# Regrouping side products, a fifth weight bank and remainders on GpSimd in a 1010-unit weight-streaming kernel

## The reference

```python
def first_block(x, ...):
    x = x + lru_mlstm_layer(rmsnorm(x, e_norm[j]), ...)   # gated linear recurrence + 4-head matrix LSTM
    x = x + ssd_layer(rmsnorm(x, o_norm[j]), ...)         # state-space layer, 8 groups of 8 heads
    return rmsnorm(x, final_norm)

def second_block(x, ...):
    proj = rmsnorm_2(x, norm_mix_w) @ w_in
    # s5_branch, gla_branch (linear attention), diff_attn_branch, mixed by sigmoid gates
    h = x + merged @ w_out
    h = h + conv_gated_mlp(rmsnorm_2(h, norm_ffn_w), ffn_w_up, ..., ffn_w_down)
    return rmsnorm_2(h, norm_final_w)
```

## Time and profile before

| | |
|---|---|
| median of 3 runs | 3103.22 us (3101.56 to 3103.56) |
| profiled execution | 3104.65 us, span 3102.9 us |
| PE busy | 3037.9 us, 98% |
| DVE busy | 2312.4 us, 75% |
| ACT busy | 1763.4 us, 57% |
| POOL busy | 540.0 us, 17% |
| DMA, mean | 181 GB/s |
| chain that ended last | PE 85%, DVE 9%, ACT 3% |

### The profile page before, as it was taken

One profiled execution on the slowest core, in us unless ns is written; L12 is line 12 of the kernel. 1 busy time (PEld: TensorE's weight loads), 2 busy tenths in 40 slices (PEclk: granted clock), 3 DMA queues, 4 the chain that ended last, 5 costly groups with the idle time before them and its releaser, 6 DMA issues.

```text
span 3102.9 us, 53505 instructions
## 1 busy us (share of the span) xinstructions
PE 3037.9 (98%) x21726; PEld 2817.8 (91%) x21726; DVE 2312.4 (75%) x3156; ACT 1763.4 (57%) x2311; POOL 540.0 (17%) x640
## 2 busy tenths in 40 slices
PE   7999999999999999999999999999999999999998
PEld 7989989889999999889888899999998888888887
DVE  7665898657888887676876888877666888887544
ACT  5554787545766776554554454445455666666442
POOL 1000000000000000145644666740001000000000
PEclk9999999999999999999999999999999999999999
DMA  5445445556565566565433445556555555555554
GB/s 215 157 155 183 159 155 183 183 190 212 189 193 184 181 190 212 195 202 197 157 136 129 157 150 173 174 178 215 187 189 188 190 190 190 189 190 190 190 189 141
DMA packets 158760, 560.49 MB, mean 181 GB/s; under 512 B 17760, under 2 KB 26016, under 8 KB 158000
## 3 DMA queue, kind: packets, MB, share of 16 engines
q1 hardware_dynamic: 158512, 557.06, 52.7%
HBM read 550.64 MB, written 6.36 MB: 180 GB/s over the span
## 4 chain that ended last, share of the span: by engine, by line
PE 85%; DVE 9%; ACT 3%; issue 1%; DMA 1%; POOL 0%; DVEq 0%; POOLq 0%; SPq 0%; ACTq 0%
PE ps L585 85%; DVE WL L1385 2%; ACT WH L940 1%; DMA RAW<-in_w 1%; ACT L923 1%; DVE XC L1359 0%; DVE XMC L1359 0%; DVE YS L1348 0%; POOL RSB L1987 0%; DVE BX L1348 0%; DVE X L1359 0%; DVE BS L1375 0%; DVE XC L1375 0%; DVE BS L1348 0%; DVE HB L1348 0%
## 5 line engine op out<-in xcount | busy, mean ns | idle before, releaser
L585 PE MATMUL ps<-XN,WH 128*128 128x256 f32 (+1 forms) x8864 | 1819.4, 299 | 12.2 <-DVE WL L1385 10.5
L940 ACT ACTIVATE WH<-RAW 128x1024 fp32r<-128x1024 f32 x1010 | 1065.5, 1058 | 1126.5 <-PE ps L585 1063.7
L1385 DVE TENSOR_TENSOR WL<-RAW,WH 128x1024 fp32r<-128x1024 f32 x1010 | 1260.2, 1254 | 457.6 <-ACT WH L940 451.2
L585 PEld LDWEIGHTS ps<-XN,WH 128*128 128x128 f32 x8864 | 1406.7, 189 | 82.0 <-issue 12.4
L585 PE MATMUL ps<-XN,WL 128*128 128x256 f32 x5120 | 1435.4, 280 | 0.0
L585 PEld LDWEIGHTS ps<-XN,WL 128*128 128x128 f32 x5120 | 967.7, 189 | 0.0
L585 PE MATMUL ps<-YS,WH 128*128 128x512 f32 (+1 forms) x1088 | 371.3, 387 | 5.9 <-DVE YS L1348 3.7
L585 PE MATMUL ps<-YS,WL 128*128 128x256 f32 x1056 | 299.1, 283 | 0.0
L1987 POOL TENSOR_TENSOR RSB<-RSB,SQ 128x256 f32<-128x256 f32 x75 | 75.5, 1007 | 1214.4 <-ACT SQ L930 1212.2
L585 PEld LDWEIGHTS ps<-YS,WH 128*128 128x128 f32 x1088 | 203.6, 189 | 48.5 <-DVE YS L1348 4.0
L585 PE MATMUL ps<-HS,WH 128*128 128x512 f32 x688 | 238.6, 390 | 0.0
(11 more groups left out here) (333 smaller groups left out, 3339.7 us busy)
## 6 DMA issues: line engine op xcount, KB each, us to landing
RAW<-in_w SPq DMA_DIRECT2D x1010, 512.0 KB, 3.3
CSB<-sums SPq DMA_DIRECT2D x64, 128.0 KB, 3.7
X<-scratch SPq DMA_DIRECT2D x2, 2048.0 KB, 7.9
X<-in_x SPq DMA_DIRECT2D x1, 2048.0 KB, 8.0
scratch<-X SPq DMA_DIRECT2D x1, 2048.0 KB, 9.4
scratch<-X SPq DMA_DIRECT2D x4, 512.0 KB, 5.9
out<-X SPq DMA_DIRECT2D x4, 512.0 KB, 2.7
X<-in_x SPq DMA_DIRECT2D x3, 512.0 KB, 8.7
```

Source lines behind the costliest of these rows:

```text
L585: return pe.e.matmul(dst, l, r, start=start, stop=stop, skip_group_check=True)
L940: act.e.activation(WH[:, w % NH, :], RAW[:, w % NB, :], ACT.Copy).then_inc(*act.one(("wh", w)))
L1385: dve.e.tensor_tensor(WL[:, w % NB, :], RAW[:, w % NB, :], WH[:, w % NH, :].bitcast(F32), SUB).then_inc(*dve.one(("wl", w)))
```

## The change

- **Gates.** The gate matrix has 32 columns instead of 36. One insertion after a head's k tiles takes its 2 q and 2 k gate products, each into 32 partitions of its own; one after its last v tile takes the 4 v gates and all 8 transposes. `gsel` sums the four groups: ScalarE copies the bank to GP, one product follows. `gates` has 10 steps.
- **Heads.** RC goes to DRAM, and for each head a DMA spreads a row over 128 partitions (RCB); the spreading product and EM go. SP waits for `den` of the head before. Later steps move by one or two.
- **State-space layer.** The products of four heads stand in one insertion, at steps 6 and 13. 23 steps. The last group starts one unit earlier, in the middle of its tile, and `HURRY` takes two steps a unit after step 15.
- **Banks.** `ring5`, after the first four tiles: banks 0 to 4 for weight tiles, 5 to 7 for side products, until `ring3` in the second block.
- **GpSimd.** WL of every fourth unit from 19 to 443 is formed there; the first tile of `w_in_2` is in unit 446.
- **Start and end.** Odd squares of the first norm on VectorE; the Silu table is loaded before the wait for the conv. At the end the last square goes into the sum by a second product, ScalarE scales X by the norm's weight beside `dn`, and four products of 128x1024 are left.
- **Others.** In `dts`, `gla`, `s5` steps of TensorE come one or two units later. Tiles narrower than 128 use 96 columns. R0 keeps its place modulo 128.

```diff
+HURRY = {("ssd", (7,)): 15}
+    p.append(Now("ring5", ()))
+            if j == 0 and g == 7:
+                p += [Part(zs, list(range(8)), True, False), Go("ssd", (g,)), Part(zs, list(range(8, 16)), False, True)]
+def by_pool(w):
+    return w % 4 == 3 and 16 <= w < THIRD
...
                     for x in evacs + beside:
                         step(x)
+                        if x in beside and x[2] > HURRY.get((x[0], x[1]), x[2]):
+                            step(x)
...
+            def gate4(four):
...
+                b = PS[holder_of("gates")]
+                for c, (kt, src) in enumerate(four):
+                    i = mm(b[32 * c:32 * c + 32, 0:256], WIF[:, kt, :], src, gates_n[0] == 0, gates_n[0] == 7)
...
+                    b = take("side", "gsum")
+                    pe.wait_ge(*at("gp"))
+                    mm(b[0:36, 0:256], cs("gsel"), GP).then_inc(*pe.one(("gsum",)))
...
                 if s == 0:
-                    b0 = take("side", "at0", h)
-                    pe.wait_ge(*at("rc"))
-                    mm(b0, ident[0:4, h:h + 1].to_broadcast([4, 128]), RC).then_inc(*pe.one(("at0", h)))
                     b1 = take("side", "at1", h)
...
-                if s in (4, 6, 9, 11):
...
+                if s in (6, 13):
+                    e_ = 4 * (s // 13)
...
+                    pe.wait_ge(*at("msk", g, e_ + 3))
+                    for n in (0, 2):
...
+            def ring5():
+                rings.update(main=[0, 1, 2, 3, 4], side=[5, 6, 7])
...
+                b = take("side", "nsum", 4)
+                pe.wait_ge(*at("sq", 4, 14))
+                mm(b[:, 0:256], ones, RSB, True, False)
+                pe.wait_ge(*at("sqr", 4, 15))
+                mm(b[:, 0:256], ones, SQ4[:, 1, :], False, True).then_inc(*pe.one(("nsum", 4)))
...
                 if s == 1 and j == 3:
+                    use(ACT.Silu)
                     act.wait_ge(*at("conv", h, 3))
...
                 square(("sqr", 4), n, RSB, 0, X[:, n, :])
+                fn(X[:, n, :], X[:, n, :], ACT.Copy, scale=cv("norm_final", n))
...
                 for w in ahead(u, AHEAD - 1):
+                    if by_pool(w):
+                        continue
                     dve.wait_ge(*at("wh", w))
...
+            def sq0(k):
+                if k % 2:
+                    if k > 2:
+                        dve.wait_ge(*at("sq", 0, k - 2))
+                    tt(SQ4[:, 1, :], X0[:, k, :], X0[:, k, :], MUL, ("sqr", 0, k))
...
-                for k in range(16):
-                    stt(X[:, k, :], X[:, k, :], cv("norm_final", k), RSB, MUL, MUL, ("fin", k // 4))
+                for k in range(4):
+                    x = X[:, 4 * k:4 * k + 4, :]
+                    tt(x, x, RSB.unsqueeze(1).to_broadcast([128, 4, 256]), MUL, ("fin", k))
...
+                    if by_pool(w):
+                        pool.wait_ge(*at("wh", w))
+                        pool.e.tensor_tensor(WL[:, w % NB, :], RAW[:, w % NB, :], WH[:, w % NH, :].bitcast(F32),
+                                             SUB).then_inc(*pool.one(("wl", w)))
...
+            def rcb(h):
+                sp.e.dma_start(RCB, rows[h:h + 1, :].to_broadcast([128, 512])).then_inc(rcb_in, 16)
+
+            def heads(s):
+                h, s = divmod(s, 16)
+                if s == 8 and h < 3:
+                    sp.wait_ge(*at("den", h))
+                    rcb(h + 1)
```

More of the change, by code:

```diff
@@ L258 @@
 assert len(ORDER) % UB == 0
+THIRD = next(n for n, x in enumerate(ORDER) if x[0] == "w_in_2") // UB
+def by_pool(w):
+    return w % 4 == 3 and 16 <= w < THIRD
 def walk(block, unit, steps):
@@ L364, in flat, with build @@
     return ap.rearrange("p a b -> p (a b)")
-def build(nc, args, out, scratch, sums):
+def build(nc, args, out, scratch, sums, rows):
     ctx = ExitStack()
@@ L679, in holder_of, with k_, v, gates @@
                 return where[user]
-            def q(h, j, s):
-                if s == 2:
[L683 to L703, removed]
+            def k_(h, j, s):
+                if s == 2 and j == 1:
+                    pe.wait_ge(*at("qd", h, 1))
+                    pe.wait_ge(*at("kd", h, 1))
+                    gate4([(2 * h + i, QKV[h][0][:, i, :]) for i in range(2)] +
+                          [(8 + 2 * h + i, QKV[h][1][:, i, :]) for i in range(2)])
+            def v(h, j, s):
+                if s != 2 or j != 3:
+                    return
+                pe.wait_ge(*at("vf", h, 3))
+                i = gate4([(16 + 4 * h + i, VF[:, i, :]) for i in range(4)])
+                if gates_n[0] == 8:
+                    i.then_inc(*pe.one(("gates",)))
+                for w in range(2):
+                    b = take("side", "vt", h, w)
+                    for t in range(2):
+                        for i in range(2):
+                            x = pe.e.transpose(b[:, 256 * t + 128 * i:256 * t + 128 * i + 128],
+                                               VF[:, 2 * w + i, 128 * t:128 * t + 128], ident)
+                    x.then_inc(*pe.one(("vt", h, w)))
+            def gates(s):
+                if s == 2:
                     kept.discard(holder_of("gates"))
-                if s == 5:
+                    b = take("side", "gsum")
+                    pe.wait_ge(*at("gp"))
+                    mm(b[0:36, 0:256], cs("gsel"), GP).then_inc(*pe.one(("gsum",)))
+                if s == 8:
                     b = take("side", "gt")
@@ L961, in sq0 @@
             def sq0(k):
-                square(("sqr", 0), k, RSB, 0, X0[:, k, :])
+                if k % 2 == 0:
+                    square(("sqr", 0), k, RSB, 0, X0[:, k, :])
             def project(L, kind, n):
@@ L2091, in x0, with gates, lru0 @@
                 load(X0[:, part, :], args["x"][:, part, :], f"x0{q}")
+            def gates(s):
+                if s == 9:
+                    sp.wait_ge(*at("rc"))
+                    load(rows, RC, "rcs")
+            def lru0():
+                sp.wait_ge(*at("rcs"))
+                rcb(0)
+            def rcb(h):
[5 more added lines that the diff above has]
+                    rcb(h + 1)
             def x1():
@@ L2195, in s5_pairs @@
 def s5_pairs(s):
-    return [(m, s - 8 - 12 * m) for m in range(16) if 0 <= s - 8 - 12 * m < 13]
+    return [(m, s - 8 - 12 * m) for m in range(16) if 0 <= s - 8 - 12 * m < 14]
 def cols(a, n):
@@ L2299, in program @@
     sums = nc.dram_tensor("sums_0", (64, 256), F32).ap()
-    build(nc, args, out, scratch, sums)
+    rows = nc.dram_tensor("rows_0", (4, 512), F32).ap()
+    build(nc, args, out, scratch, sums, rows)
 def kernel(**inputs):
```

204 lines of the change are left out of this document (103 added, 101 removed), and 4 rows, old and new, of the table STEPS.

## The result

The changed kernel takes 3147.39 us (median of 4 runs, 3141.34 to 3151.60), the kernel before 3102.39 us beside it: ratio 1.014, 95% interval 1.0128 to 1.0152. It is slower by 1.4%, where 3069 us was forecast, and outside the range of 3046 to 3091 us. Its profiled execution has 3141.34 us, 36.7 us more than the one of before.

A forecast was written before the change was run, and what follows sets the result against it. The prediction took TensorE, busy for 98% of the span, as the bound. Savings on its stream and waits, less 1 us lost, summed to 33.9 us: from 3103.2 to 3069 us, range 3046 to 3091 us.

The forecast's parts named there:

- The WL products on GpSimd: Moving 107 WL products from VectorE to POOL: gains and losses sum to zero (-12 to +12), 1 us lost elsewhere.
- 466 us is still under 542 us: From 718 to 1260 us: VectorE's 444 us plus 43 moves at 0.5 us fit the stretch, so they are hidden.
- the signs named ahead: Signs of error: VectorE's busy time nearing the stretch (718 to 1260 us), growing waits for WL, POOL's mean over 3.2 us.
- A: VectorE blocked for POOL's whole product, 11 units from 400 to 547 us: 17 us lost, 3086 us; chance 0.2.
- D: Slower than before because POOL's 128x1024 product takes far longer: at 4.5 us each, 3148 us; chance 0.05.
- B: Stalls from 400 to 547 us vanish, 11 us, and the lower clock with them, 2.9 us: 3055 us; chance 0.17.
- C: The four gate products do not go side by side, so 10.3 us come back: 3079 us; chance 0.07.
- E: TensorE's gains come back as waits of other chains in all stages: 3102 us; chance 0.03.
- Later steps: dt, decay and state products one or two units later: all 2.2 us of GE waits saved (-3 to +5).
- Three side banks: Last users of side banks are done two steps before, so no cost; without that cover 0.7 us a group, 6 us.
- The start: First norm, half the squares moved from ScalarE to VectorE: 2.0 us saved (0 to 4); following stretch 2.5 us (1 to 4).
- End of layer 2: Last state-space group earlier: YS wait and lower clock saved, new wait of 1.6 us, net 3.8 us (2 to 5.4).

The follow-up runs named there:

- r5: Kernel before, with only the move of every fourth unit's WL to GpSimd: 3152.53 us, ratio 1.0161 to before.
- r1: Changed kernel with all WL products back on VectorE: 3096.52 us, ratio 0.9975 to before.
- r10: r7 with the four gate products of an insertion one after the other in one group of 32 columns: 3086.57 us.
- r4: Changed kernel with the edits of r1, r2 and r3 together: 3079.72 us, ratio 0.9919 to before.
- r3: Changed kernel with the steps of gla, diff and s5 where they were before: 3133.08 us, ratio 1.0089 to before.
- r9: Changed kernel with the edits of r1 and r3 together, five weight banks kept: 3078.35 us, ratio 0.9914 to before.
- r2: Changed kernel with four banks for weight tiles and four for side products throughout: 3139.32 us, ratio 1.0115 to before.
- r7: r4 with all sixteen squares of the first norm on ScalarE: 3077.94 us, ratio 0.9918 to before.
- r8: r7 with the last state-space group started and stepped as before: 3081.31 us, ratio 0.9932 to before.
- r11: r7 with the fifth weight bank in units 8 to 56 alone: 3073.12 us, ratio 0.9899 to before.

## Why the prediction was wrong

**The WL products on GpSimd, counted zero (-12 to +12), cost 51 us.** This step failed. Its price for POOL was right: the product took 2.41 us in the median (2.51 in the mean) for the 2.4 forecast. VectorE's loss was even smaller than forecast. In units 242 to 342, before and then after, all engines and L1385 or L1417 (WL) alone:

```profile
778.29:1088.73 310.44, 310.44 (x2632) 300.92 (x2631) 263.71 (x375) 213.65 (x275) 10.16 (x10) 1.00 0.58 187
778.29:1088.73 310.44, 120.89 (x100) 1.00 0.58 187
```

```profile
781.19:1100.02 318.83, 309.80 (x2632) 301.39 (x2631) 265.80 (x351) 212.47 (x277) 72.48 (x35) 1.00 0.57 182
781.19:1100.02 318.83, 90.02 (x76) 1.00 0.57 182
```

25 WL products moved there. VectorE's WL time fell by 30.9 us, and its other work grew from 142.8 to 175.8 us, 33 us, for the same number of operations. So a moved product held VectorE up for 1.3 us and spared it 1.2, a loss of 0.1 us each (0.2 in r5), where the forecast took 0.5 and 1.2 as the bound. What failed is the conclusion from it, that "466 us is still under 542 us" and the moves are therefore hidden. A sum of busy time says that VectorE can catch up within a layer. It doesn't say that a chain (XV, Silu, RS, bank) meets its due unit, and that is what TensorE waits for. Units 222 to 362 lose 13 us where nothing was counted, 88 to 160 lose 16 us (all after less r1), and 400 to 446, a stretch the forecast did not look at, 9.5 us. In that last stretch it is the other way round: WL itself is late. All of TensorE's idle time there, 5.9 us, is three waits for POOL's WL; the rest lies in the clock (0.98) and in smaller differences. At one of them POOL's product ran for 3.32 us beside VectorE's, at two it stood in POOL's queue behind small products of s5 (PB, PT).

Of the signs named ahead, one came: waits for WL grew, from 12.5 us to 25.8 us for VectorE's and 10.3 us for POOL's. Much of the first is not POOL's doing, since r1 has 20.4 us. VectorE's busy time did not near the stretch, and POOL's mean stayed under 3.2 us.

**Rivals.** A named the mechanism, VectorE blocked by POOL, but priced it by VectorE's busy time and for 11 units in one stretch (17 us); after is slower than r1 in every stretch with moved units but 160 to 222, where the two are equal within 0.2 us. D had the time, 3148 us, by luck, since its mechanism did not occur: POOL needed 2.4 to 2.5 us and not over 3.7. B fell: the stretch from 400 to 547 us has clock 0.93 and a TensorE that is busy for less, 129.73 us against 135.88. C fell by r10, and E by r4: the gains of TensorE's stream stay gains once the three losses are out.

**Later steps, +2.2 forecast, cost about 14 us** (after against r3; 18 us by r1 against r9). Units 464 to 560 take 368.0 us against 351.1, and 560 to 656 give 2.9 us of it back, which no run explains. 12.8 us are the waits for ST and SC, the rest lies mainly in the clock behind them. The GE waits went, as forecast. The bound of -3 named the right place, one unit of margin for two, and was about five times too small: it is near one such wait (2.5 us), and there are four for ST, one of 4.1 us for SC, and the clock.

**Three side banks, counted nothing.** That their last users are done two steps before holds only while VectorE isn't held up: 1.8 us of waits for RS in r1, 11.5 in after. The bound of 0.7 us a group for lost cover was too small there: r2 gets 6.1 us back in five groups, 1.2 each.

**The start, +2.0 forecast, gave -2.5:** TensorE waits 9.4 us for RSB, before 6.7. POOL still adds fifteen squares, and with VectorE's squares among them its last addition ends at 42.1 us, before at 39.3. The sign was wrong; r7 is near 0. The 2.5 us counted for the stretch behind it (the table load, a WL less on VectorE, Q gates that don't wait) did not come: TensorE stands 3.7 us in units 8 to 56 before and 4.9 in r7. It stands 1.9 in r1, where the fifth bank is the main difference.

**End of layer 2, +3.8 forecast, gave -0.4** (r8): the wait for YS went and that for POOL's SQ came, 3.0 us for the 0 to 3 expected. What was missed, by my reading of r8, is that the chain's own steps stand two units later.

**What was right.** By the unit table, r7 against before: units 8 to 56 gain 13.6 us, as the gates' sum had it (r10 confirms the 10.3 us of it that come from side by side), and the sum of four groups costs 1.2 us (0.7 forecast). Row broadcast and EB's margin gain 6.3 us in 88 to 160 (2.0 forecast, 4.2 the bound; EB's waits were counted elsewhere). 4.9 us of it are busy time of TensorE and only 1.4 are waits: those for EB went, but 8.1 us for ZB came in r7. The state-space groups gain 5.3 us in 222 to 362, as forecast; one insertion takes 1.45 us from its first product to the stream's next (784.08 to 785.53):

```profile
784.08 1.52 PE L601 MATMUL ps<-DB,XDT 128*64 128x256 f32 x16
785.53 0.50 PE L601 MATMUL ps<-XN,WH 128*128 128x256 f32 x2
```

The tail gains 4.2 us (after is 40.8 us behind at the last unit and 36.6 at the end), as forecast. VectorE's last row in after, against the earlier trace rows:

```profile
3131.30 5.00 DVE L1378 TENSOR_TENSOR X<-X,RSB 128x1024 f32<-128x1024 f32 x4 [2.19 <-ACT RSB L956]
```

The fifth bank, counted nothing, gains 3.3 us in units 8 to 56, and about as much is lost with it elsewhere.

**Together.** Without its two large losses the change gains 27 us (r9 against before), the later steps cost 18 us (r1 against r9) and the WL products 51 us (after against r1). That is 42 us of the 45 us measured. No run undoes the narrower tiles or the place of R0.

## What to carry to other kernels

Don't offload to GpSimd by busy shares. Here, moving a product between SBUF tiles from VectorE to GpSimd freed 1.2 us of VectorE and took up to 2.2 us from whatever stood there then; ask which chain that is and when TensorE is due to use it. A product that nobody needs, run there on purpose, measures the price (0.55 us each here) before anything is moved. And when a regrouping shifts the steps of a chain, count the units between the last producer and its user at every hand-over, since a margin of one unit did not hold where two did.

## What the runs showed of the hardware

**The same small waits come with different clocks.** r4 and the kernel before wait alike from unit 446 to 560 (BS 3.6, GE 2.2 or 2.3, OB 2.2, DS 1.3 us), yet r4 takes 6.3 us longer. Before (the columns as above):

```profile
1400.40:1804.90 404.50, 394.53 (x2817) 358.54 (x2816) 314.17 (x414) 212.11 (x310) 223.00 (x280) 1.00 0.46 156
```

r4:

```profile
1378.00:1788.80 410.80, 400.73 (x2818) 363.25 (x2816) 314.47 (x414) 212.03 (x310) 222.11 (x280) 0.98 0.46 153
```

TensorE is idle for 10.0 us in one and 10.1 in the other, but the granted clock is 1.00 and 0.98. It isn't the code either: with the same steps there, r3 and r11 take 404.5 us, r7 406.1, and r9 410.8. What decides it, no run shows. So 6 us between two versions can be the clock alone, and a gain of that size needs its stretch shown.

**An operation of VectorE with one tensor operand is held up too.** TENSOR_SCALAR XV<-XP,CV took up to 2176 ns for its 414 beside POOL; in r1 none of the 48 takes over 417. And POOL's products run 2.36 us at the least and 3.41 at the most for the same 128x1024: it too is delayed at times. By what, no run here separates.
